# The gate projection's two tiles behind the first keys, receptances and values; the first preparation at step 18

## The reference, cut to what matters

```python
P = u @ w_in                       # z | xbc | dt | r k v wd ad gd
pr = pr + (prev - pr) * mu         # prev: pr one token earlier
logw = -softplus(-(w0 + tanh(wd) @ w2)) - 0.5
decay = exp(-exp(logw))
a = sigmoid(a0 + ad @ a2)
g = sigmoid(gd) @ g2
kk = normalised(k * k_k);  k = k * (1 + (a - 1) * k_a)
y = wkv7_scan(r, decay, k, v, -kk, kk * a)
y = group_norm(y) + bonus;  return y * g
```

## Time and profile before

| | us |
|---|---|
| median of 3 runs | 2993.31 |
| lowest, highest | 2992.87, 2995.45 |
| the profiled execution's own time | 2990.47 |
| its span, first to last instruction | 2988.6 |
| PE (TensorE matmul) busy | 2854.9 |
| VectorE, ScalarE, GpSimd busy | 2113.4, 1564.1, 773.4 |
| mean granted TensorE clock, as a share of full speed | 0.983 |

### The profile page before, as it was taken

One profiled execution on the slowest core, in us unless ns is written; L12 is line 12 of the kernel. 1 busy time (PEld: TensorE's weight loads), 2 busy tenths in 40 slices (PEclk: granted clock), 3 DMA queues, 4 the chain that ended last, 5 costly groups with the idle time before them and its releaser, 6 DMA issues.

```text
span 2988.6 us, 53223 instructions
## 1 busy us (share of the span) xinstructions
PE 2854.9 (96%) x21346; PEld 2554.0 (85%) x21346; DVE 2113.4 (71%) x3407; ACT 1564.1 (52%) x2611; POOL 773.4 (26%) x942
## 2 busy tenths in 40 slices
PE   8977999999999998899899999998999999999998
PEld 8867988888888888888788888997888888888887
DVE  7888887765777666677777776777676665566654
ACT  6445565543555555465555655455445444444443
POOL 0465422110111221666365540001021110011112
PEclk9898999999999999999999999999999999999999
DMA  6312555556555565322222223454555555655554
GB/s 256 133 43 97 171 186 196 184 178 191 205 188 190 175 198 192 128 89 93 89 93 93 100 100 107 155 181 152 172 190 188 186 195 172 207 186 196 180 181 148
DMA packets 79828, 475.39 MB, mean 159 GB/s; under 512 B 8224, under 2 KB 11296, under 8 KB 38304
## 3 DMA queue, kind: packets, MB, share of 16 engines
q1 hardware_dynamic: 76768, 459.66, 44.7%
q10 hardware_dynamic: 2816, 12.32, 1.2%
HBM read 465.66 MB, written 6.29 MB: 158 GB/s over the span
## 4 chain that ended last, share of the span: by engine, by line
PE 77%; DVE 13%; ACT 4%; POOL 3%; issue 3%; DMA 0%; SPq 0%; ACTq 0%; POOLq 0%; DVEq 0%
PE bank L727 36%; PE bank L731 23%; PE bank L729 5%; PE bank L730 5%; DVE m L1257 3%; ACT m L2184 2%; DVE m L1303 1%; POOL m L2919 1%; POOL m L2915 1%; DVE m L1582 1%; DVE m L1963 1%; PE bank L1063 1%; PE bank L743 1%; PE bank L1174 0%; PE bank L1067 0%
## 5 line engine op out<-in xcount | busy, mean ns | idle before, releaser
L731 PE MATMUL bank<-m,m 128*128 128x256 f32 x6864 | 1929.0, 281 | 0.0
L727 PE MATMUL bank<-m,m 128*128 128x512 f32 x4736 | 1649.5, 393 | 6.9 <-DVE m L2058 5.7
L1257 DVE TENSOR_TENSOR m<-m,m 128x1024 fp32r<-128x1024 f32 (+1 forms) x944 | 1072.5, 1145 | 581.6 <-ACT m L2184 575.3
L731 PEld LDWEIGHTS bank<-m,m 128*128 128x128 f32 x6864 | 1299.1, 189 | 0.2
L2184 ACT ACTIVATE m<-m 128x1024 fp32r<-128x1024 f32 (+1 forms) x944 | 911.0, 979 | 672.2 <-PE bank L731 648.1
L727 PEld LDWEIGHTS bank<-m,m 128*128 128x128 f32 x4736 | 890.8, 188 | 206.7 <-DVE m L2058 5.9
L729 PE MATMUL bank<-m,m 128*128 128x256 f32 x2128 | 633.9, 298 | 31.4 <-DVE m L1257 25.1
L730 PE MATMUL bank<-m,m 128*128 128x256 f32 x2128 | 603.7, 284 | 0.0
L729 PEld LDWEIGHTS bank<-m,m 128*128 128x128 f32 x2128 | 408.5, 192 | 55.0 <-issue 42.6
L730 PEld LDWEIGHTS bank<-m,m 128*128 128x128 f32 x2128 | 409.1, 192 | 1.5
L2895 POOL TENSOR_TENSOR m<-m,m 128x256 fp32r<-128x256 f32 x44 | 63.4, 1441 | 547.7 <-ACT m L2461 547.7
(11 more groups left out here) (388 smaller groups left out, 2871.1 us busy)
## 6 DMA issues: line engine op xcount, KB each, us to landing
m<-in_w_up SPq DMA_DIRECT2D x88, 1024.0 KB, 4.7
m<-in_w_down SPq DMA_DIRECT2D x128, 704.0 KB, 4.0
m<-in_w_gu SPq DMA_DIRECT2D x88, 1024.0 KB, 4.8
m<-in_w_out SPq DMA_DIRECT2D x48, 1024.0 KB, 5.1
m<-in_w_krv SPq DMA_DIRECT2D x48, 1024.0 KB, 4.8
m<-in_w_xbc SPq DMA_DIRECT2D x24, 1024.0 KB, 4.8
m<-in_w_z SPq DMA_DIRECT2D x16, 1024.0 KB, 4.7
m<-in_w_in SPq DMA_DIRECT2D x14, 1024.0 KB, 6.2
```

The costliest lines, as they stand in the source:

```text
L727: pe.matmul(bank.rearrange("p (a b) -> p a b", a=2), hi, x, start=kc == L.k0, stop=False)
L731: m = pe.matmul(ps, lo, x[:, 0, :], start=False, stop=last)
L1257: v.tensor_tensor(lo_of(k), raw_of(k)[0], hi_of(k).bitcast(F32), SUB).then_inc(*lo_v(("lo", k)))
```

## The change

The four small tiles become two and two: `L_sm` keeps decay and rate, in banks 0 and 1, and the gate's tiles (`L_gd`) are computed behind `L_krv[0]`, also in banks 0 and 1. Names of the evacuations (`raw`) are renumbered to that order. The first two preparations begin at steps 18 and 46 instead of 24 and 44 (`FIRST`); the later ones stay. The first preparation's bank waits for the last residual of the layer before instead of the evacuation of a small tile. VectorE's `prep` has one more wait, for the shift of the receptances that it multiplies in place.

```diff
--- before.py
+++ after.py
@@ -185,6 +185,7 @@
 
 
 AFTER, PAIRS, ROUNDS, STEPS = 24, 56, 20, 100
+FIRST = (18, 46)
 
 
 def second_mixer(main, block, tail, after, *early):
@@ -194,7 +195,7 @@
         return timed(*((PAIRS + ROUNDS * b + 5 * e, chain(block(2 * b + e, 0), block(2 * b + e, 1))) for b in range(8)))
 
     tails = timed(*((PAIRS + ROUNDS * (i // 2 + 1) + 5 * (i % 2), tail(i)) for i in range(16)))
-    afters = timed(*((AFTER + ROUNDS * b, after(b)) for b in range(8)))
+    afters = timed(*((FIRST[b] if b < 2 else AFTER + ROUNDS * b, after(b)) for b in range(8)))
     run(mix((main, 5), (heads(0), 1), (heads(1), 1), (tails, 1), (afters, 1), *((g, 1) for g in early)))
 
 
@@ -591,7 +592,7 @@
             L_up.append(linear("w_up", 44, 16, FOUR, lambda t: ffn_v["sum", t], t0=44 * q, wide=True))
             L_down.append(linear("w_down", 16, 44, FOUR, lambda t, q=q: res_v["down", q, t], k0=22 * q, k1=22 * q + 22,
                                  wide=True))
-        L_sm = linear("w_sm", 4, 16, FOUR, lambda t: wkv_v["raw", t], step=1)
+        L_sm = linear("w_sm", 2, 16, TWO, lambda t: wkv_v["raw", t], step=1)
         L_krv, L_g2, L_x = [], [], []
         turn = [TWO, TWO[::-1]]
 
@@ -604,8 +605,10 @@
         for b_ in range(8):
             if b_ >= 4:
                 g2(b_ - 4)
-            L_krv.append(linear("w_krv", 6, 16, turn[0] if b_ else (4, 5), lambda t: wkv_v["raw", 4 + t], t0=6 * b_,
-                                step=1))
+            L_krv.append(linear("w_krv", 6, 16, turn[0] if b_ else (4, 5),
+                                lambda t: wkv_v["raw", 4 + t if t >= 6 else 2 + t], t0=6 * b_, step=1))
+            if b_ == 0:
+                L_gd = linear("w_sm", 2, 16, TWO, lambda t: wkv_v["raw", 6 + t], t0=2, step=1)
         g2(4)
         L_bc = linear("w_xbc", 8, 16, turn[0], lambda t: ssd_v["raw", t], t0=16, step=1)
         g2(5)
@@ -957,7 +960,7 @@
                 if i >= 2:
                     pe.wait_ge(*wkv_v["xa", i // 2 - 1, e])
                 else:
-                    pe.wait_ge(*wkv_v["raw", 2 + e])
+                    pe.wait_ge(*res_v["down", 1, 14 + e])
                 if i >= 6:
                     for k in range(2):
                         pe.wait_ge(*wkv_v["out", i // 2 * 2 - 6 + k])
@@ -1108,9 +1111,10 @@
 
             def main():
                 two = nrhs, lambda kc: cut_of(N_two, kc)
-                yield from linear(L_sm, *two, free=[[res_v["down", 1, 12 + n]] for n in range(4)])
+                yield from linear(L_sm, *two, free=[[res_v["down", 1, 12 + n]] for n in range(2)])
                 yield from linear(L_krv[0], *two)
-                yield from linear(L_krv[1], *two, free=[[wkv_v["raw", 0]], [wkv_v["raw", 1]]])
+                yield from linear(L_gd, *two, free=following(L_sm))
+                yield from linear(L_krv[1], *two, free=following(L_gd))
                 for b in range(2, 4):
                     yield from linear(L_krv[b], *two, free=following(L_krv[b - 1]))
                 for b in range(4, 8):
@@ -1733,7 +1737,8 @@
                     *wkv_v(("sh", x), name))
 
             def small(t):
-                raw_shift(L_sm, t, bank_of(L_sm, t))
+                L = L_sm if t < 2 else L_gd
+                raw_shift(L, t, bank_of(L, t))
                 if t == 0:
                     R = slice(96, 128)
                     v.wait_ge(*wkv_v.last)
@@ -1814,6 +1819,7 @@
                 v.wait_ge(*wkv_a["pi", i])
                 v.tensor_copy(PL[:, i, :].unsqueeze(2), pb[:, :, 32:33]).then_inc(*wkv_v())
                 r4 = AR(i)[:, :, 1, :].rearrange("p s (a b) -> p s a b", b=32)
+                v.wait_ge(*wkv_v["krv", 6 * (i // 2) + 2 + i % 2])
                 v.tensor_tensor(r4, r4, pb[:, :, 1:33].rearrange("p (s a) b -> p s a b", s=2), MUL).then_inc(*wkv_v())
                 yield
                 v.wait_ge(*wkv_a["ka", i])
@@ -1976,6 +1982,8 @@
                     if b >= 4:
                         yield from linear(L_g2[b - 4], gated)
                     yield from linear(L_krv[b], krv)
+                    if b == 0:
+                        yield from linear(L_gd, small)
                 yield from linear(L_g2[4], gated)
                 yield from convolved(L_bc)
                 yield from linear(L_g2[5], gated)
@@ -2921,7 +2931,7 @@
                         yield
 
             def main():
-                yield from linear(L_sm, small)
+                yield from linear(L_sm)
                 for b in range(8):
                     if b == 0:
                         g.wait_ge(*norm_v["lo", N_two.x0 + 15])
```

## The result

In 22 runs each the changed kernel takes 2998.56 us (2991.63 to 3001.82), the kernel before 2993.73 (2990.93 to 2997.55): ratio **1.0014**, 95% interval 1.0008 to 1.0020. By the ratio that is +4.2 us, where -3.9 was forecast. The profiled execution has a span of 2993.9 us, its own time is 2995.65.

The account below looks back on a forecast made before the run. TensorE, busy 96%, was taken as the bound, with winnable time in the second mixer's first 55 steps. Starting the head block of step 56 16.9 us earlier, less 13.0 of losses, gave -3.9: 2989.4 us, range 2981 to 2999.

Parts of the forecast that it names:

- rival 3: At L964, step 18: copies land at 1172.9, 11 us of PE wait replaces the one removed; +7.6 us, slower; chance 0.13.
- PE without the wait at 1161.9: Preparation 0, step 18: PE would reach L964 at 1161.9, with two weight stalls gone and thirty blocks fewer ahead.
- L964 at 1169.4: Preparation 0's first matmul, step 18: starts at 1169.4 after a new 7.5 us PE wait for a2; copies issued near 1158.0.
- The queue of SP loads keeps its number and pace: Tile order part: reordering the small tiles leaves the SP load queue unchanged; the order's cost was put at zero.
- 11.4 us for the copies: Copies of w2 and a2 before L964: 11.4 us to land, as measured before, kept against a skill-page estimate of 8.0.
- Clock behind the wait, 1.7: PE after the 7.5 us wait at step 18: one half-clock stretch, loss 1.7 us (0 to 3.4).
- Gates 2.5: Gate tiles' sigmoids, now at steps 29 and 32: loss 2.5 us (0.5 to 3.0), before 3.04.
- Preparation 0, 2.5: Stalls and clock in preparation 0: loss 2.5 us (1.0 to 4.6), its table load coming while PE waits for a2.
- Preparation 1, 5.5: Preparation 1 beside GpSimd's first solve, ending near 1251: loss 5.5 us (2.0 to 9.8), before 9.8.
- First transpose 0: VectorE's standstill at L1843, reached near 1255, 4 us after GpSimd's end: loss 0 (up to 3), before 5.02 plus 1.9 clock.
- Second transpose 0.8: Transpose at step 72, with preparation 1 two steps later: VectorE stands 1.6 us, PE's share 0.8 (0 to 3).
- rival 1: Preparation 1 runs free: a2 lands early, GpSimd ends while most of preparation 1 is still to come; -12.3 us; chance 0.22.

Follow-up runs that it names:

- e5: Changed kernel, with the w2 and a2 columns preparation 0 needs copied at step 0 into an idle buffer, full copies at step 26: 2982.91 us, 0.9964 to before.
- e3: Changed kernel, with the first two pairs' decay and rate matmuls on resident constants, so nothing there waits for w2 and a2: 2986.47 us, 0.9976 to before.
- e4: Changed kernel, with w2 and a2 each copied in two parts, first the 256 columns that preparation 0 needs: 2993.16 us, 1.0002 to before.
- e7: Kernel before, old tile order, with only the first two preparations moved to steps 22 and 46: 2986.69 us, 0.9980 to before.
- e1: Changed kernel with the first preparations left at steps 24 and 44, so only the tile order is new: 3004.65 us, 1.0036 to before.
- e2: Kernel before, old tile order, with preparation 1 alone moved from step 44 to 46: 2990.9 us, 0.9989 to before.
- e11: The early-copy version (e5) with preparation 1 left at step 44 instead of 46: 2984.52 us, 0.9970 to before.

## Why the prediction was wrong

It had the mechanism and the place: a wait for `a2` on PE, with a stretch at half clock behind it. Its size decides between the forecast and rival 3, and the size was off: the save that comes ahead of the copies was forecast too early and too short. Point by point, times of after less 4.0 us:

- **PE without the wait at 1161.9:** right. e5 shows 1162.0.
- **L964 at 1169.4: this step failed.** It came at 1174.6, 5.2 late, by two terms of the working. The first is when the second save goes out: at 1155.4, only 1.8 us earlier than before, where 3.9 was forecast. The forecast set the *evacuation* of tile 3 before (1154.78) against the *end* of the tile, and 1150.7 is where the tile ended before as well (1152.29 less the stall of 1.60 behind it). Its evacuation came 1.7 us earlier, and VectorE scales the last chunks of h behind it (VectorE's timeline of the changed kernel, 4.0 us to be taken off):

```profile
1157.06 0.42 DVE L1726 TENSOR_TENSOR m<-bank,m 128x256 f32<-128x256 f32 x1
...
1158.46 0.88 DVE L1345 SCALAR_TENSOR_TENSOR m<-m,m,m 128x256 f32<-128x256 f32 x2
```

  With 4.3 us for the save that alone would have put the copies at 1159.7 instead of 1158.0. The second term is the save itself. "The queue of SP loads keeps its number and pace" holds, but the working took the save's time from before, 4.3 us, and it took 7.5. The loads keep their pace against PE, but the saves were moved against the loads. The load of 1 MB of weights that precedes it on SP's queue is now issued 1.2 us ahead of the first save (1150.38 and 1151.56), where it was 3.4 us ahead before; the first save took 8.9 us instead of 5.2 and the second 7.5 instead of 4.3. In all kernels with the new order but e3 the first save takes 8.0 to 9.2 us and the second 5.1 to 8.2, in those with the old 5.1 to 5.3 and 4.1 to 4.3. In e3's execution the load went out 2.1 us ahead of the first save (1150.23 and 1152.34), and the saves took 5.5 and 4.2. That fits the distance to the load as the cause, but it is my reading of these rows; no run moved the save alone. So the copies went out at 1162.9 (forecast 1158.0): 1.7 us for the save's place and 3.2 for its length. They landed 11.6 us later (forecast 11.4). My upper bound, 1172.9, "if the copies go out no earlier than before", left out that they may go out later than before. Rival 3 decides from a landing of about 1172 on, and the landing was at 1174.4. It comes nearest: it had 11 us of wait, 9.8 for preparation 1 and +7.6 in all, against 11.2, 7.1 and +4.2.
- **11.4 us for the copies:** right, against the estimate of 8.0 by the Trainium skill ("DMA: Bandwidth & Descriptors", section "Anatomy of one DMA — SWDGE (gpsimd) path"). Its fit of 2.0 us plus bytes over 436 GB/s gives an estimate of 2.2 us for 96 KB: e5 agrees (2.1 and 2.4), e4 does not (8.1, with loads and the rest of the copies beside it). The page fits it to copies issued from GpSimd; these come from ScalarE's queue.
- **Clock behind the wait, 1.7:** 1.8, half of the 3.55 busy us of the second row below.
- **Gates 2.5:** 1.19.
- **Preparation 0, 2.5:** 1.05+0.45+0.41 of stalls and 1.7 of clock, 3.6. The table load, which I had put into the wait, came at 1184.75, behind it.
- **Preparation 1, 5.5:** a stall of 4.25 and 2.9 of clock, 7.1. "GpSimd's system 0 ... ends near 1251" failed. It was handed over at 1208.4 and ended at 1264.1, and even its length was wrong: 55.8 us instead of 49.8.
- **First transpose 0:** VectorE stood 1.63 us, PE not at all.
- **Second transpose 0.8:** VectorE stood 0.45; from step 56 to step 76 it is 66.8 us instead of 65.0, so 1.8, in PE stalls of 0.58, 0.85 and 1.16.

Windows of the changed kernel (columns as above) for the clock rows, the counterpart of the earlier trace rows:

```profile
1172.00:1178.60 6.60, 0.00 (x0) 0.00 (x0) 0.00 (x0) 0.00 (x0) 0.00 (x0) 0.50 0.75 178
1178.60:1182.20 3.60, 3.55 (x9) 2.87 (x10) 0.00 (x0) 0.00 (x0) 0.00 (x0) 0.50 0.02 5
...
1189.10:1192.50 3.40, 3.40 (x18) 3.40 (x18) 1.50 (x6) 2.31 (x5) 0.00 (x0) 0.50 0.44 118
...
1264.20:1271.00 6.80, 5.71 (x87) 5.67 (x88) 4.52 (x8) 2.84 (x4) 3.27 (x10) 0.50 0.22 92
```

PE stands for the whole of the first window and 3.6 us of the next go at the lower level. The last one is preparation 1.

The misses add up: +5.2 (wait) +0.1 (clock) -1.3 (gates) +1.1 (preparation 0) +1.6 (preparation 1) +1.0 (second transpose) = +7.7, and 0.4 up to step 56 that these rows don't place; -3.9+8.1 = +4.2, which is what the mixer shows at step 76 and what the ratio gives. That the ratio agrees so closely is in part chance, since the profiled execution wins back 3 us later and lies 2.9 us under the median. The range (2981 to 2999) held the median, 0.4 us from its end, only because it took in most of rival 3; the forecast's sign did not hold.

Two thirds of the error is the wait. The other misses come to +2.9 and would by themselves have left a gain of 1.0 (-3.9+2.9), if they don't hang on the wait, which no run shows. That the wait as a whole turns a gain into a loss is shown by e3 and e5: with it gone the same order and the same steps are 12 and 15 us faster than the change, 7 and 10 faster than before. That is on the way to rival 1's -12.3, but not by its mechanism: rival 1 wanted preparation 1 free of GpSimd, and in e5 it is not (3.85 us of stall); e5 gains by starting 12.6 us earlier.

## What to carry to other kernels

When a consumer is moved ahead, follow its inputs back to their first issue, and ask of every transfer on that chain what will be under way beside it after the move, since a duration from the old trace belongs to its old neighbours. If the input is small, issue it where little else moves data, into a buffer that is idle just then, as e5 does; making it smaller in its crowded place (e4) shortened the wait by 1 us. And two engines that slow each other are to be placed against each other in time: the steps at which work begins, two integers here, were worth 6 us by themselves (e7), of the 10 that the best kernels gained.

## What the runs showed of the hardware that was not expected

**VectorE slows GpSimd, too.** The solve's 62 ops are the same before and after. The POOL groups in the stretch from the hand-over to VectorE's next transpose, before and then after (count, busy us, mean ns, idle):

```profile
L2919 POOL TENSOR_TENSOR m<-m,m 128x31 f32<-128x31 f32 (+15 forms) x31 | 21.6, 695 | 2.4
L2915 POOL TENSOR_TENSOR m<-m,m 128x31 f32<-128x31 f32 (+15 forms) x31 | 20.9, 673 | 2.4
```

```profile
L2925 POOL TENSOR_TENSOR m<-m,m 128x31 f32<-128x31 f32 (+15 forms) x31 | 23.8, 767 | 2.4
L2929 POOL TENSOR_TENSOR m<-m,m 128x31 f32<-128x31 f32 (+15 forms) x31 | 23.7, 766 | 2.4
```

And what VectorE did in these stretches (the third busy time is DVE's; the windows of before, then of after):

```profile
1208.30:1256.90 48.60, 39.04 (x369) 38.01 (x367) 30.71 (x45) 21.11 (x32) 43.54 (x64) 0.93 0.32 109
```

```profile
1213.70:1268.30 54.60, 48.82 (x457) 47.56 (x456) 39.42 (x56) 27.65 (x42) 49.54 (x65) 0.96 0.44 155
```

Before, VectorE worked 30.7 of 48.6 us, since it stood for 8.87 us at the end; after, 39.4 of 54.6. One op shows it: 128x135 on GpSimd takes 0.42 us while VectorE stands and 1.36 beside a weight remainder of VectorE, here on POOL's timeline, before and then after:

```profile
1252.66 0.42 POOL L2915 TENSOR_TENSOR m<-m,m 128x135 f32<-128x135 f32 x1
```

```profile
1218.30 1.36 POOL L2925 TENSOR_TENSOR m<-m,m 128x135 f32<-128x135 f32 x1
```

So the standstill that the change was to remove had been paying part of itself back. VectorE's standstill and the length of GpSimd's first solve go together over the kernels: 8.88 and 49.6 us in e1, 4.60 and 50.9 in e2, 2.04 and 52.8 in e7, 1.63 and 55.8 in the changed kernel. It isn't the standstill alone: in e11 VectorE stands 4.02 us, nearly as in e2, and the solve takes 54.4. A solve can't be taken at its old length once VectorE does other work beside it.

**The time varies more in the changed kernel.** Its 22 runs spread over 10.2 us, e4's over 17.0, e5's five over 3.3. In the changed kernel and in e4 PE waits some 10 us for a DMA, and the save before it differs between executions with the new order (the second takes 7.5 and 8.2 us there, 5.1 in e11). But e1 spreads over 11.8 us in six runs without such a wait, so a landing that varies isn't the whole cause; what is stays open.
